# Differential attention of a two-stack transformer: scores, softmax, values and head norm of each pair of heads moved between the projections

## The reference, cut to what matters

```python
qkv = h @ w_qkv                       # q, k, v: 1024 columns each
q = qkv[..., :qk_w].reshape(B, S, 16, 64); k = ...; v = qkv[..., 2*qk_w:].reshape(B, S, 8, 128)
q = apply_rope(q, cos, sin) * 64 ** -0.5
k = apply_rope(k, cos, sin)
s = einsum('bhqd,bhkd->bhqk', q, k)
p = softmax(s).reshape(B, 8, 2, S, S)
a = p[:, :, 0] - lam * p[:, :, 1]     # two softmaxes for each of 8 heads
o = einsum('bhqk,bhkd->bhqd', a, v)
o = rms_norm(o, subln) * (1.0 - lambda_init)     # over the 128 values of each head
return o @ w_o                        # x = x + this, then the SwiGLU
```

## Time and profile before

| what | us |
|---|---|
| median of three executions | 2483.61 |
| profiled execution, device time | 2479.64 |
| its span on the core | 2477.8 |
| PE busy in the span | 2343.1 (95%) |
| DVE busy | 1551.1 (63%) |
| ACT busy | 1136.9 (46%) |

### The profile page before, as it was taken

One profiled execution on the slowest core, in us unless ns is written; L12 is line 12 of the kernel. 1 busy time (PEld: TensorE's weight loads), 2 busy tenths in 40 slices (PEclk: granted clock), 3 DMA queues, 4 the chain that ended last, 5 costly groups with the idle time before them and its releaser, 6 DMA issues.

```text
span 2477.8 us, 45807 instructions
## 1 busy us (share of the span) xinstructions
PE 2343.1 (95%) x18358; PEld 2251.9 (91%) x18358; DVE 1551.1 (63%) x2028; ACT 1136.9 (46%) x1477; POOL 344.3 (14%) x448
## 2 busy tenths in 40 slices
PE   8899998999999999999989998988999999889998
PEld 8799997699999999999979998887889988868998
DVE  6746547465466766654775554677677557866763
ACT  4643344543345554433464333534355453445552
POOL 0002100012000000220301210560011019000110
PEclk9989998999999999999998999987999999989999
DMA  6327543166544444665533754433346543524651
GB/s 225 120 70 203 186 143 110 52 168 181 183 158 149 143 150 141 170 186 185 167 103 96 192 184 148 129 102 136 103 137 185 187 137 120 166 70 121 186 187 68
DMA packets 431038, 362.12 MB, mean 146 GB/s; under 512 B 20524, under 2 KB 404144, under 8 KB 430904
## 3 DMA queue, kind: packets, MB, share of 16 engines
q1 hardware_dynamic: 429128, 358.79, 47.3%
q0 software_dynamic: 1264, 0.71, 0.1%
q10 hardware_dynamic: 512, 0.72, 0.1%
HBM read 359.12 MB, written 1.05 MB: 145 GB/s over the span
## 4 chain that ended last, share of the span: by engine, by line
PE 82%; DVE 7%; POOL 6%; ACT 3%; issue 1%; DMA 0%; SPq 0%; ACTq 0%; DVEq 0%; POOLq 0%
PE bank L449 72%; POOL hT L1273 4%; POOL Z L1275 2%; DVE weights_lo L1775 2%; PE bank L480 2%; PE bank L552 2%; PE bank L775 1%; ACT weights_hi L1311 1%; PE bank L789 1%; PE bank L487 1%; PE bank L687 1%; PE bank L905 1%; PE bank L937 1%; PE bank L918 1%; DVE negmax L1990 1%
## 5 line engine op out<-in xcount | busy, mean ns | idle before, releaser
L449 PE MATMUL bank<-h_hi,weights_hi 128*128 128x256 f32 (+1 forms) x3856 | 1115.1, 289 | 48.8 <-DVE h_lo L2221 16.6
L1775 DVE TENSOR_TENSOR weights_lo<-weights,weights_hi 128x2048 fp32r<-128x2048 f32 x343 | 790.2, 2304 | 553.3 <-ACT weights_hi L1311 551.4
L449 PE MATMUL bank<-h_lo,weights_hi 128*128 128x256 f32 (+1 forms) x3856 | 1105.5, 287 | 0.0
L449 PE MATMUL bank<-h_hi,weights_lo 128*128 128x256 f32 (+1 forms) x3856 | 1105.0, 287 | 0.0
L1311 ACT CAST weights_hi<-weights 128x2048 fp32r<-128x2048 f32 x343 | 652.8, 1903 | 573.3 <-PE bank L449 564.4
L449 PEld LDWEIGHTS bank<-h_hi,weights_hi 128*128 128x128 f32 (+1 forms) x3856 | 754.1, 196 | 58.6 <-issue 43.5
L449 PEld LDWEIGHTS bank<-h_lo,weights_hi 128*128 128x128 f32 (+1 forms) x3856 | 754.1, 196 | 1.5 <-issue 1.4
L449 PEld LDWEIGHTS bank<-h_hi,weights_lo 128*128 128x128 f32 (+1 forms) x3856 | 753.6, 195 | 0.0
L449 PE MATMUL bank<-hid_hi,weights_hi 128*128 (+1 forms) x1056 | 295.4, 280 | 0.0
L449 PE MATMUL bank<-hid_lo,weights_hi 128*128 (+1 forms) x1056 | 295.4, 280 | 0.0
L449 PE MATMUL bank<-hid_hi,weights_lo 128*128 (+1 forms) x1056 | 295.4, 280 | 0.0
(11 more groups left out here) (299 smaller groups left out, 2478.1 us busy)
## 6 DMA issues: line engine op xcount, KB each, us to landing
weights<-in_f_w_gu SPq DMA_DIRECT2D x176, 512.0 KB, 5.0
weights<-in_f_w_out SPq DMA_DIRECT2D x88, 512.0 KB, 4.2
weights<-in_w_up SPq DMA_DIRECT2D x88, 512.0 KB, 4.9
weights<-in_w_in SPq DMA_DIRECT2D x82, 512.0 KB, 4.4
weights<-in_c_w_qkv SPq DMA_DIRECT2D x72, 512.0 KB, 4.5
weights<-in_a_w_qkv SPq DMA_DIRECT2D x48, 512.0 KB, 4.7
weights<-in_w_down SPq DMA_DIRECT2D x44, 512.0 KB, 4.0
weights<-in_a_w_o SPq DMA_DIRECT2D x16, 512.0 KB, 3.9
```

Source lines behind the costliest of these rows:

```text
L449: mm = nc.tensor.matmul(out, x, y, start=(first and n == 0), stop=(last and n == 2), skip_group_check=True)
L1775: v_.tensor_tensor(w_lo[slot][:], raw[slot][:], w_hi[slot][:].bitcast(F32), ALU.subtract).then_inc(lo_ready, 1)
```

## The change

In `attn_a` the stage of attention is gone. The units are put in the order q0 k0 v0 q1 k1 q2 k2 v1 q3 k3 v2 v3, where the number is the pair of heads, so that a pair can start as soon as its own projections are there. Each unit is split in two halves, counted as steps: step t = 2n + half, for the 12 units and then the four of the output projection (steps 24 to 31). After a half TensorE does what the tables hold for that step. For the heads 0 to 7 these are the scores at steps 6, 7, 12, 13, 16, 17, 21, 22; the difference (VectorE) two steps after the scores; the transposes (`turn`) three steps after them; the values at steps 11, 12, 17, 18, 23, 24, 26, 27. The sums of squares of each pair stand one step after the values of its second head (13, 19, 25, 28), the spreading one step after that (14, 20, 26, 29). VectorE and ScalarE go through the same steps, with their refills among them. The head norm is thus done for each pair on its own, with four roots in place of one. Scores of all heads use the banks 4 and 7, transposes bank 6, values bank 5. `oA_lo` and two small tiles are new.

```diff
+A_UNITS = [("q", 0), ("k", 0), ("v", 0), ("q", 1), ("k", 1), ("q", 2), ("k", 2), ("v", 1), ("q", 3), ("k", 3),
+           ("v", 2), ("v", 3)]
+A_WO = 2 * len(A_UNITS)
+A_SCORES_AT = {6: 0, 7: 1, 12: 2, 13: 3, 16: 4, 17: 5, 21: 6, 22: 7}
+A_SCALE_AT = {s + 2: hd for s, hd in A_SCORES_AT.items()}
+A_TURN_AT = {s + 3: hd for s, hd in A_SCORES_AT.items()}
+A_VALUES_AT = {11: 0, 12: 1, 17: 2, 18: 3, 23: 4, 24: 5, 26: 6, 27: 7}
+A_STATS_AT = {s + 1: hd // 2 for s, hd in A_VALUES_AT.items() if hd % 2}
+A_SPREAD_AT = {s + 1: pair for s, pair in A_STATS_AT.items()}
+A_STATS_BANK, A_SPREAD_BANK = (2, 2, 4, 4), (3, 3, 7, 7)
...
# TensorE
+                def scores(hd):
+                    pe.wait_ge(rot_ready, rot0 + 2 * (hd // 2) + 2)
+                    S[hd] = [open_item(4), open_item(7)]
+                    for tt in range(NT):
+                        for z, s in enumerate(S[hd]):
...
+                def between(t):
+                    if t in A_SCORES_AT:
+                        scores(A_SCORES_AT[t])
+                    if t in A_TURN_AT:
+                        turn(A_TURN_AT[t])
+                    if t in A_VALUES_AT:
+                        values(A_VALUES_AT[t])
+                    if t in A_STATS_AT:
...
+                        for hh in range(2):
+                            mm = stats(s.bank, 2 * hh, sq, [4 + hh])
...
+                    if t in A_SPREAD_AT:
...
+                        pe.wait_ge(rs_ready, count(rs_ready))
...
+                wo("a_w_o", l, (i, "wo"), 0, src=(o_hi, oA_lo), between=lambda n, half: between(A_WO + 2 * n + half))
...
# ScalarE
+                for t_ in range(A_WO + 8):
+                    n, half = t_ // 2, t_ % 2
+                    if half and n < len(A_UNITS):
...
+                        evict(n)
+                    if t_ in A_TURN_AT:
...
+                        free(nc.scalar.copy(expoAT[hd % 2], banks[6][:]), TT[hd])
+                    if t_ in A_SCORES_AT:
...
+                    if t_ in A_VALUES_AT and A_VALUES_AT[t_] % 2:
...
+                    if t_ in A_STATS_AT:
...
+                        free(fn(std_heads[:, 4 * g:4 * g + 4], banks[s.bank][:, 0:4], ACT.Sqrt, scale=1.0 / P,
+                                bias=eps[:, 0:1]), s)
...
+                    if half and n < len(A_UNITS):
+                        refill(us[n])
...
# VectorE
+                for t_ in range(A_WO + 8):
+                    n, half = t_ // 2, t_ % 2
+                    if t_ in A_SCORES_AT:
+                        maxima(A_SCORES_AT[t_])
+                    if t_ in A_STATS_AT:
...
+                        v_.reciprocal(rs_heads[:, 4 * g:4 * g + 4], std_heads[:, 4 * g:4 * g + 4]).then_inc(rs_ready, 1)
+                    if t_ in A_SPREAD_AT:
...
+                        done(b)
+                        free(v_.scalar_tensor_tensor(sq[:, 6:8, :], oT, subg[:, l:l + 1],
...
+                    if half == 0 and n:
...
+                            swap_rotate(xs[n - 1], qT[:, m:m + 2, :], hT[:, 0, :], hT[:, 1, :], SWAP_8)
+                        if n <= len(A_UNITS) + 3:
+                            refill((us + wo_units)[n - 1])
+                    if t_ in A_SCALE_AT:
+                        difference(A_SCALE_AT[t_])
+                    if t_ in A_SPREAD_AT:
+                        split(A_SPREAD_AT[t_])
```

More of the change, by code:

```diff
@@ L482, in stats, with spread @@
                 return mm
-            def spread(bank, at, col):
+            def spread(bank, at, col, rs=rs):
                 for tt in range(NT):
@@ new lines, in scores @@
+                def scores(hd):
[3 more added lines that the diff above has]
+                        for z, s in enumerate(S[hd]):
+                            a = HD * z
+                            mm = nc.tensor.matmul(banks[s.bank][:, tt * T:(tt + 1) * T], qT[a:a + HD, hd, tt * P:(tt + 1) * P],
+                                                  qT[a:a + HD, KT + hd, :], start=True, stop=True)
+                            if tt:
+                                close(mm, s)
@@ new lines, in attn_a @@
+                for n, (kind, pair) in enumerate(A_UNITS):
+                    u = next_unit(block_loads("a_w_qkv", l, 1024 * "qkv".index(kind) + 256 * pair))
+                    w = parts(u, 256)
+                    x = open_item(n % 2)
+                    x.pre = n % 3
+                    if n == 0:
+                        close(tiles(halves(x.bank), w, (0, P), h, gate=gate), x, u)
+                    for half in range(2):
+                        if kind == "v":
+                            mm = token_major(halves(x.bank)[half], w, slice(0, 256), half)
+                        elif n:
+                            mm = tiles([halves(x.bank)[half]], w, (half * P,), h)
+                        if half and n:
+                            close(mm, x, u)
+                        between(2 * n + half)
@@ L713, in attn_a @@
                     if n < 2:
                         (norm_sums, norm_spread)[n]()
+                    xs.append(x)
+                    if kind == "v":
+                        vs.append(x)
                     us.append(u)
[L716 to L720 removed]
@@ new lines, in attn_a, with evict @@
+                rotated = count(rot_ready, len(rotations)) - len(rotations)
+                norm_deviation()
+                def evict(n):
+                    kind, pair = A_UNITS[n]
+                    x = xs[n]
+                    done(x)
+                    if kind == "v":
+                        for tt in range(NT):
+                            ins = fn(vA[:, tt, 256 * pair:256 * pair + 256], pair_of(x)[:, tt, :], ACT.Identity,
+                                     scale=rs[:, tt:tt + 1], bias=eps[:, 3:4])
+                        free(ins, x)
+                    else:
+                        before = [r for r, m in enumerate(rotations) if m < n and xs[m].pre == x.pre]
+                        if before:
+                            act.wait_ge(rot_ready, rotated + before[-1] + 1)
+                        free(fn(pre[x.pre][:], banks[x.bank][:], ACT.Copy, scale=HD ** -0.5 if kind == "q" else 1.0), x)
@@ L1444, in probs_t @@
+                    if t_ in A_SPREAD_AT:
+                        g = A_SPREAD_AT[t_]
+                        freed(items[i, "spreads"][g])
+                        nc.scalar.copy(o_hi[:, 2 * g:2 * g + 2, :], sq[:, 6:8, :]).then_inc(hi_part, 1)
+                    if half and n < len(A_UNITS):
+                        refill(us[n])
+                    elif half and n < len(A_UNITS) + 3:
+                        refill(wo_units[n - len(A_UNITS)])
+                late.append(wo_units[3])
             def probs_t(hd, TT):
@@ L2008, in attn_a, with maxima @@
-                s, sp_items = items[i, "subln"]
-                freed(s)
-                v_.reciprocal(rs[:, 0:16], std[:, 0:16]).then_inc(rs_ready, 1)
-                for g in range(5):
-                    if g < 4:
-                        b = sp_items[g]
+                def maxima(hd):
+                    for z, s in enumerate(S[hd]):
+                        done(s)
+                        v_.tensor_reduce(negmax[(2 * hd + z) % 4][:], banks[s.bank][:].rearrange("p (m n) -> p m n", m=2), AX.X,
+                                         ALU.max, negate=True).then_inc(negmax_ready, 1)
```

229 lines of the change are left out of this document (92 added, 137 removed).

## The result

Ten executions of the kernel after have a median of 2490.29 us (2488.43 to 2497.14), beside ten of the kernel before at 2483.99. The ratio is 1.0029, with a 95% interval of 1.0019 to 1.0039: the change costs 0.3%, some 6 to 7 us. The forecast was 2492. One of the ten executions before took 3246.68 us; it was a slow one and stands in the median but not in the ratio. The profiled execution took 2488.43 with a span of 2486.6, against 2479.64 and 2477.8 before.

What follows compares the result with a forecast made beforehand. PE was taken as the bound. To the profiled 2479.64 us came 0.7 for blocks and waits against the old stage and 7.4 for the clock, 2487.7; with 3.97 up to the median, 2492. Range of the likeliest case: 2484 to 2498.

Steps and rivals of the forecast that it cites:

- The bound: Whole kernel: PE, busy 95% of the span; what is late next is VectorE, by its order and not its load.
- The waits: PE's waits in one pass of the changed attention, from walking three engines' orders step by step: 16.9 us.
- The blocks: PE's attention work between halves of units, scores, values, transposes, sums and spreading: 30.9 us a pass.
- that of the values: Price of one head's block of values in a pass: 1.22 us, eight times.
- The 0.37 of switching: Part of the price of each block of values, read from dilated attention: 0.37 us on top of 0.85 streaming.
- The clock: PE's loss to the lower clock behind the waits of 4.9 and 3.2 us: 2.4 and 1.3, 3.7 us a pass.
- that inference from one row: In dilated attention a wait of 2.4 us left the clock at 1.00; only the two longest waits were charged.
- The sum: Whole kernel: 8.1 us more, +0.7 for blocks and waits and +7.4 for the clock; 2492 as a median.
- the clock holds: Rival: the waits come in both passes but cost no clock; +0.7 us, 2484; chance 0.28.
- a switch costs two loads' worth: Slower rival: each ScalarE table switch holds 1.28 us more at four places a pass; 2502 with clock; chance 0.06.
- the waits are as short as in dilated attention: Faster rival: PE waits only at the end of a pass, 2.4 us; 28.3 us less, 2455; chance 0.08.
- Eight table loads more in the program: ScalarE's table loads go from two to six a pass; the four more cost it 5.1 us.

Runs made afterwards that it cites:

- difference first: Kernel after with VectorE's difference at the head of its step, ahead of maxima, scaling, rotation and refill; 2464.32 us.
- transposes later: Kernel after with transposes four steps behind the scores, not three, VectorE's order unchanged; 2463.66 us.
- filled: Kernel after with idle matmuls, results unread, ahead of three waits a pass (transposes of heads 0 and 2, last output unit); 2481.53 us.
- scaling last: Kernel after with VectorE's scaling of a pair moved behind rotation, refill and difference in its step; 2481.41 us.
- no roots: Kernel after with the head norm's four roots replaced by Identity, so heads are not normed rightly; 2477.9 us.
- both: Kernel after with the edits of difference first and transposes later together; 2457.64 us.
- two more banks: Kernel of both, with scores of odd heads in banks 2 and 3, sums and spreading in 4 and 7; 2452.41 us.
- the same, again: Kernel of two more banks, unchanged, run again as a reference beside and its bank; 2456.05 us.
- log and exp: Kernel of two more banks, with the inverse root taken as exp(-0.5 ln x) on ScalarE, without VectorE's reciprocal; 2458.41 us.
- spreading later: Kernel of two more banks, with the spreading of pair 0 one step later, in step 15 instead of 14; 2460.77 us.
- and its bank: Kernel of spreading later, with pair 0 spread into bank 3 instead of bank 7; 2457.0 us.
- The first two experiments: The kernels difference first and transposes later, each one edit to the kernel after; 2464.32 and 2463.66 us.

## Why the prediction was right, and where it was not

The table sets the passes side by side, each from the start of unit 2 to the sums of the next norm, as the traces have them, first pass / second pass. The last column is the length less the waits and less half of the time at the lower clock.

| kernel | pass, us | PE's waits | at half clock | what is left |
|---|---|---|---|---|
| before | 133.2 / 136.1 | 10.5 / 9.7 | 13.7 / 20.5 | 115.8 / 116.2 |
| after | 137.3 / 138.5 | 17.0 / 17.0 | 13.7 / 13.7 | 113.5 / 114.6 |
| difference first | 126.8 / 125.4 | 8.8 / 9.8 | 6.8 / 0 | 114.6 / 115.6 |
| transposes later | 123.4 / 125.6 | 8.3 / 8.5 | 0 / 3.4 | 115.1 / 115.4 |
| filled | 132.4 / 133.0 | 8.2 / 8.4 | 0 / 0 | 124.2 / 124.6 |
| scaling last | 134.5 / 135.0 | 15.0 / 15.0 | 10.2 / 10.2 | 114.4 / 114.9 |
| no roots | 134.7 / 135.3 | 13.2 / 13.2 | 13.7 / 13.7 | 114.7 / 115.3 |
| both | 121.6 / 122.2 | 7.0 / 7.1 | 0 / 0 | 114.6 / 115.1 |
| two more banks | 118.7 / 119.2 | 4.4 / 4.4 | 0 / 0 | 114.3 / 114.8 |
| the same, again | 118.8 / 120.7 | 4.4 / 4.4 | 0 / 3.4 | 114.4 / 114.6 |
| log and exp | 121.5 / 122.1 | 5.7 / 5.7 | 3.4 / 3.4 | 114.1 / 114.7 |
| spreading later | 123.9 / 124.6 | 7.4 / 7.4 | 6.8 / 6.8 | 113.1 / 113.8 |
| and its bank | 122.0 / 121.4 | 4.6 / 4.6 | 6.8 / 3.4 | 114.0 / 115.1 |

But for the kernel with fillers, which carries 72 matmuls of 0.12 us more (9 us), what is left lies between 113.1 and 115.6 us. So two terms, PE's waits and its clock, account for the passes of eleven traces to about 1 us. (Where a low stretch lies partly inside a wait, half of it is too much; with that part left out the range is 113.9 to 115.6 us, and the kernel before has 116.0 and 116.6.)

This also says what the change did. Against the kernel before it took 1.1 and 1.2 us of work off the passes and 1.2 and 3.7 us of loss to the clock, and it added 6.5 and 7.3 us of waits: 4.2 and 2.4 us more.

**The bound.** Right: PE, and the order of VectorE's queue rather than its load. The fastest variant has the same busy time of VectorE and waits 4.4 us.

**The waits.** Right in sum, 17.0 for 16.9, and nearly so one by one, forecast first: transposes of head 0 3.2 and 3.0, of head 2 4.9 and 4.85, of head 4 0.8 and 1.3, of head 5 0.8 and 0.8; spreading 1.4 and 1.6; scores of heads 5 and 7 1.1 and 1.4 against 1.2 and 1.3, of head 1 0.5 and 0.15; of head 6 0.6 and 0.5; the last unit 2.3 and 2.3. The first two experiments show the cause that was named. The walk through three queues, with durations from rows of the other stages, was worth the trouble: no total of busy time gives these numbers.

**The blocks.** Too dear: 30.9 us a pass were forecast. What is left of both passes when 80.6 us of projections, 17.0 of waits and the loss to the clock (below) are taken off is 28.6 and 28.5. The mis-sized term is that of the values. Timeline of PE in the kernel after, values of head 0:

```profile
64.80 0.28 PE L466 MATMUL bank<-h_hi,weights_lo 128*128 128x256 f32 x1
64.92 1.02 PE L746 MATMUL bank<-hT,V 128*128 128x256 f32 x4
65.60 0.47 PE L466 MATMUL bank<-h_hi,weights_hi 128*128 128x256 f32 x1
65.90 0.28 PE L466 MATMUL bank<-h_lo,weights_hi 128*128 128x256 f32 x1
```

From 64.80 to 65.90 less two steps of 0.12 are 0.86 us, where 1.22 stood in the sum. The 0.37 of switching was taken over from dilated attention, and it is not paid here, but for one block of values inside the output projection, which costs 1.17. The others came closer: scores 1.26 for 1.27, transposes 0.44 for 0.48, sums 0.89 for 0.95, spreading 0.90 for 0.84. These prices are those of blocks without a pause. With a pause a block costs more than its price and the idle time (scores 1.33, spreading 1.15), for which the sum had nothing.

**The clock.** Too cheap: 3.7 us a pass were charged, the fillers bought back 5.0 and 5.5. From the windows of the first pass, counting what of a low stretch PE did not wait: around the transposes of head 0 (3.4 less 0.6 inside the wait) / 2 = 1.4 for 1.3; around head 2 (6.8 less 2.1) / 2 = 2.3 for 2.4; and 3.4 / 2 = 1.7 from 158.8 on, behind the wait of 2.3 us for `oA_lo`, which was charged nothing, since 2.4 us had left the clock alone in dilated attention. That is 5.4, and in the second pass, where less of the stretches lies inside the waits, 6.1. The step that failed is that inference from one row.

**The sum.** 132.1 us were forecast from unit 2 to the last output matmul, 131.6 and 132.2 are there: 2.3 and 2.4 too much for the blocks, 1.7 and 2.4 too little for the clock, 0.1 too little for the waits. So the passes came out to half a microsecond in part by luck, by errors of opposite signs. (The single waits on record add up to 17.1 with the one at unit 3, not to 16.9, and that one is not in the trace.) The total was forecast 8.1 higher; it measured +7.4 in the passes, +8.8 in spans and +6.3 in medians.

**The rivals.** That the clock holds (2484) fell by the windows. That a switch costs two loads' worth fell by the rows of ScalarE. That the waits are as short as in dilated attention (2455) was wrong for this kernel, but names what it lacks: with one more step before the transposes it takes 2463.66, with the difference first as well 2457.64. Eight table loads more in the program, 40 for 32, and six a pass for two: right, and five of the six are gone without the roots.

**What would be kept.** The kernel with two more banks beats both kernels, in two groups of runs, by 1.31% and 1.16% of the kernel before. The idea of the change is sound, and its order of work takes the gain away.

## What to carry to other kernels

When work is moved between the halves of dense units, cost it by walking each engine's queue in order and noting what stands ahead of the instruction for which the bound engine asks. A refill or a wait ahead of a small dependent step is worth more than any of the step's own durations; put the dependent step first, or ask for it one step later. Before a producer is moved later, look at what its bank and the casts behind it keep others from doing: a wait is easily passed on at the same size. And where the bound engine must stand still, count what its clock loses behind the wait as a second term, here a third of the wait itself.

## What the runs showed of the hardware that was not expected

**A wait of one length, two clocks.** The kernel with two more banks was traced twice. In both traces PE waits 2.31 us for `oA_lo` in the second pass, until 1301.17 in one and until 1299.91 in the other. Windows of the 4 us behind the wait, the first from the one trace and the second from the other:

```profile
1301.17:1305.17 4.00, 4.00 (x34) 4.00 (x35) 3.03 (x3) 0.98 (x2) 0.00 (x0) 1.00 0.46 127
...
1299.91:1303.91 4.00, 4.00 (x23) 4.00 (x24) 2.89 (x2) 0.98 (x2) 0.00 (x0) 0.64 0.50 134
```

The same instructions behind the same wait run at full clock in one execution and partly at half in the other. Over the passes of all thirteen traces, a stretch at half clock began in or within 1.5 us behind each of the 18 waits of 2.8 us and more, 10 of the 22 waits of 2.3 us and 5 of the 10 of 1.8 us, and none of the 16 of 1.6 us. So a wait between 1.8 and 2.3 us may or may not cost clock, and no run here tells what decides.

**The same code, up to 8 us apart.** Windows from the end of the second pass to the end of the span, in the kernel with two more banks:

```profile
1313.17:2449.70 1136.53, 1055.72 (x8110) 1013.14 (x8108) 737.70 (x961) 510.00 (x639) 232.27 (x266) 0.95 0.47 142
```

and in its second set of runs:

```profile
1313.46:2457.70 1144.24, 1065.57 (x8110) 1018.54 (x8108) 736.95 (x961) 509.69 (x638) 231.31 (x266) 0.94 0.47 141
```

The same instructions take 7.7 us longer, at a granted clock of 0.94 and not 0.95. That is nearly all of the difference between the two profiled executions (2451.55 and 2459.53). Over all traces the parts outside the passes take 2208 to 2218 us, though no experiment changes them. Differences of less than some 5 us between two variants are therefore better read from the lengths of the passes than from whole times; the passes of this kernel agree to 0.1 us in the first and 1.5 in the second.
